# Turning the head outputs on VectorE instead of TensorE in the first stack of a two-stack kernel

## The reference

```
h = rms_norm(x, gain);  proj = h @ w_in          # q, k, v, z of two kinds of attention, and two gates
DA: 8 heads, two maps each:  a = softmax(q1 k1') - lam * softmax(q2 k2');  o = rms_norm(a @ v) * c
    ua = o * silu(z)                             # 256 columns a head
SB: 16 heads of 128:  w = stick-breaking weights of q k';  ub = (w @ v) * silu(z)
y = sigmoid(gate_a) * (ua @ w_branch_a) + sigmoid(gate_b) * (ub @ w_branch_b)
x = x + y @ w_out
```

## Time and profile before

| what | value |
|---|---|
| median of 3 runs | 3218.58 us (3218.3 to 3219.7) |
| span of the profiled execution | 3216.8 us, 1.8 us less than the median of the runs |
| TensorE busy | 3208.1 us, 100% of the span |
| VectorE busy | 2002.6 us, 62% |
| ScalarE busy | 1666.2 us, 52% |
| GpSimd busy | 502.8 us, 16%; 424.81 us of it in the first 1650 us |
| TensorE transposes of U, L2075 | 128, in 32 groups of four |
| granted TensorE clock | 1.000 over the whole span |

### The profile page before, as it was taken

One profiled execution on the slowest core, in us unless ns is written; L12 is line 12 of the kernel. 1 busy time (PEld: TensorE's weight loads), 2 busy tenths in 40 slices (PEclk: granted clock), 3 DMA queues, 4 the chain that ended last, 5 costly groups with the idle time before them and its releaser, 6 DMA issues.

```text
span 3216.8 us, 47383 instructions
## 1 busy us (share of the span) xinstructions
PE 3208.1 (100%) x16986; PEld 2760.8 (86%) x16986; DVE 2002.6 (62%) x2267; ACT 1666.2 (52%) x2326; POOL 502.8 (16%) x425
## 2 busy tenths in 40 slices
PE   9999999999999999999999999999999999999999
PEld 7888888888888888888888888888889999999997
DVE  6667655555544555666654555444458888688975
ACT  5445455555444444454455555444446557465663
POOL 4544500000000003445410000000001000100000
PEclk9999999999999999999999999999999999999999
DMA  6555555554555555455555455555564444544454
GB/s 241 174 171 183 173 174 169 176 171 168 191 195 192 193 196 185 164 187 171 170 178 179 165 175 174 183 192 194 192 209 166 155 144 147 181 160 162 145 182 146
DMA packets 157289, 568.95 MB, mean 177 GB/s; under 512 B 17552, under 2 KB 19744, under 8 KB 156768
## 3 DMA queue, kind: packets, MB, share of 16 engines
q1 hardware_dynamic: 155680, 558.00, 52.1%
q0 software_dynamic: 1488, 9.26, 0.8%
HBM read 565.09 MB, written 2.10 MB: 176 GB/s over the span
## 4 chain that ended last, share of the span: by engine, by line
PE 99%; POOL 1%; DVE 0%; issue 0%; ACT 0%; DVEq 0%; POOLq 0%; ACTq 0%
PE acc L1955 23%; PE acc L1957 23%; PE acc L1956 23%; PE acc L2343 5%; PE acc L2344 5%; PE acc L2345 5%; PE acc L2270 1%; PE acc L2268 1%; PE acc L2269 1%; PE work L2018 1%; PE work L2406 1%; PE work L2314 1%; PE work L2317 1%; PE work L2318 1%; PE work L2373 0%; PE work L2432 0%
## 5 line engine op out<-in xcount | busy, mean ns | idle before, releaser
L1181 DVE TENSOR_TENSOR w_lo<-raw,w_hi 128x1024 fp32r<-128x1024 f32 x1055 | 1400.2, 1337 | 992.2 <-ACT w_hi L663 858.4
L663 ACT ACTIVATE w_hi<-raw 128x1024 fp32r<-128x1024 f32 x831 | 873.4, 1057 | 903.9 <-PE acc L1957 898.7
L1955 PE MATMUL acc<-w_hi,hT_hi 128*128 128x512 f32 x2560 | 1013.7, 396 | 1.4 <-DVE hT_lo L1187 1.4
L1957 PE MATMUL acc<-w_hi,hT_lo 128*128 128x512 f32 x2560 | 998.1, 390 | 0.0
L1956 PE MATMUL acc<-w_lo,hT_hi 128*128 128x512 f32 x2560 | 996.6, 389 | 0.0
L1957 PEld LDWEIGHTS acc<-w_hi,hT_lo 128*128 128x128 f32 x2560 | 480.5, 188 | 102.6
L1955 PEld LDWEIGHTS acc<-w_hi,hT_hi 128*128 128x128 f32 x2560 | 481.0, 188 | 96.2 <-issue 1.7
L1956 PEld LDWEIGHTS acc<-w_lo,hT_hi 128*128 128x128 f32 x2560 | 481.4, 188 | 95.5
L677 ACT ACTIVATE w_hi<-raw 128x1024 fp32r<-128x1024 f32 x224 | 236.1, 1056 | 260.1 <-PE acc L2345 200.1
L2343 PE MATMUL acc<-h_hi,w_hi 128*128 128x272 f32 (+1 forms) x1088 | 318.5, 293 | 0.0
L2344 PE MATMUL acc<-h_lo,w_hi 128*128 128x272 f32 (+1 forms) x1088 | 311.9, 287 | 0.0
(11 more groups left out here) (381 smaller groups left out, 3830.4 us busy)
## 6 DMA issues: line engine op xcount, KB each, us to landing
raw<-weights SPq DMA_DIRECT2D x1056, 512.0 KB, 3.4
mat<-mats POOLq DMA_DIRECT2D x2, 1536.0 KB, 8.7
X<-x_in SPq DMA_DIRECT2D x8, 256.0 KB, 8.1
GB_rows<-rows POOLq DMA_DIRECT2D x1, 2048.0 KB, 9.9
out<-out_rows SPq DMA_DIRECT2D x8, 256.0 KB, 2.6
par<-params POOLq DMA_DIRECT2D x2, 640.0 KB, 5.4
cst<-consts POOLq DMA_DIRECT2D x1, 704.0 KB, 6.2
cst<-consts POOLq DMA_DIRECT2D x1, 552.0 KB, 5.1
```

The source lines that it names most:

```text
L663: act.activation(w_hi[:, slot, :], raw[:, slot, :], ACT.Copy).then_inc(hi_ready, 1)
L1181: dve.tensor_tensor(w_lo[:, s % RING, :], raw[:, s % RING, :], w_hi[:, s % RING, :], ALU.subtract)\
L1955: pe.matmul(o, stat[0][:, kc, token], hi, start=(kc == 0), stop=False)
L1957: ins = pe.matmul(o, stat[1][:, kc, token], hi, start=False, stop=(kc == KC - 1))
```

## The change

TensorE's `turn_u` is removed, and with it the wait of `turn_qk` for `u_lo`. VectorE gets a `turn_u` of its own directly after `make_u`: sixteen stream transposes for each unit. Transpose (i, j) reads 32 partitions of U, with 32 columns of each of four blocks (two column halves by two token tiles), turns each 32 x 32 block, and writes 32 x 128 values to the partitions 32 j of a new SBUF tile `UT`. `UT` lies where the score tile `SM` is, which holds nothing that is still needed at that time. U is stored in another order of its free axes, and `make_u` of an SB pair is two instructions instead of one. `u_hi` waits for all sixteen transposes and reads `UT` in SBUF instead of PSUM, and so does `u_lo`.

The diff at its core:

```diff
+        sm_at = mem.at
         SM = mem.place("SM", [P, 2, 384])
+        UT = mem.place("UT", [P, 4, 4, 32], at=sm_at)
-        U = mem.place("U", [P, NT, 256])
+        U = mem.place("U", [P, 2, NT, P])
...
             def u_hi(m):
-                act.wait_ge(uT_turned, m["n"] + 1)
+                act.wait_ge(uT_turned, 16 * (m["n"] + 1))
-                act.activation(dst[:, bass.ds(2 * m["i"], 2), :], work[:, 0, :].rearrange("p (c n) -> p c n", c=2), ACT.Copy)\
-                    .then_inc(uT_hi, 1)
+                act.activation(dst[:, bass.ds(2 * m["i"], 2), :].rearrange("p c (t i r) -> p (c t) i r", t=NT, i=4),
+                               UT[:, :, :, :].rearrange("p i b r -> p b i r"), ACT.Copy).then_inc(uT_hi, 1)
...
+            def turn_u(m):
+
+                dve.wait_ge(u_ready, 2 * (m["n"] + 1))
+                for i in range(4):
+                    for j in range(4):
+                        dve.transpose(UT[32 * j:32 * j + 32, i, :, :],
+                                      U[32 * i:32 * i + 32, :, :, 32 * j:32 * j + 32].rearrange("p c t n -> p (c t) n")).then_inc(uT_turned, 1)
...
             def u_lo(m):
-                dve.tensor_tensor(lo[:, c, :], work[:, 0, :].rearrange("p (c n) -> p c n", c=2), hi[:, c, :], ALU.subtract)\
-                    .then_inc(uT_lo, 1)
+                tokens = "p c (t i r) -> p (c t) i r"
+                dve.tensor_tensor(lo[:, c, :].rearrange(tokens, t=NT, i=4), UT[:, :, :, :].rearrange("p i b r -> p b i r"),
+                                  hi[:, c, :].rearrange(tokens, t=NT, i=4), ALU.subtract).then_inc(uT_lo, 1)
...
                 split(u, 12, 13 + late)
                 if prev:
                     make_u(prev)
+                    turn_u(prev)
                 split(u, 13 + late, 16)
...
-                pe.wait_ge(uT_lo, m["n"])
                 for a in range(4):
...
-            def turn_u(m):
-                pe.wait_ge(u_ready, 2 * (m["n"] + 1))
-                for c in range(2):
-                    for t in range(NT):
-                        o = c * SEQ + t * P
-                        ins = pe.transpose(work[:, 0, o:o + P], U[:, t, c * P:c * P + P], ident)
-                ins.then_inc(uT_turned, 1)
...
-                halves(u, hT, 9 + late, 13 + late)
-                if prev:
-                    turn_u(prev)
-                halves(u, hT, 13 + late, 16)
+                halves(u, hT, 9 + late, 16)
```

More of the change, by code:

```diff
@@ L689, in layer_start @@
                     act.wait_ge(const_set, 2)
-                    act.activation(small[:, 90:91], U[:, 0, 0:1], ACT.Copy)
+                    act.activation(small[:, 90:91], U[:, 0, 0, 0:1], ACT.Copy)
                     act.wait_ge(set_loaded, 32)
@@ L1290, in make_u @@
                     for t in range(NT):
-                        dve.scalar_tensor_tensor(U[:, t, :], work[:, 1, 256 * t:256 * t + 256], o_rstd[:, t:t + 1],
-                                                 ZG[:, t, :], ALU.mult, ALU.mult).then_inc(u_ready, 1)
+                        dve.scalar_tensor_tensor(U[:, :, t, :], work[:, 1, 256 * t:256 * t + 256].rearrange("p (c n) -> p c n", c=2),
+                                                 o_rstd[:, t:t + 1], ZG[:, t, :].rearrange("p (c n) -> p c n", c=2),
+                                                 ALU.mult, ALU.mult).then_inc(u_ready, 1)
                 else:
                     dve.wait_ge(av_ready, m["n"] + 1)
-                    dve.tensor_tensor(U[:, :, :], work[:, 1, :].rearrange("p (t n) -> p t n", t=2), ZG[:, :, :], ALU.mult)\
-                        .then_inc(u_ready, 2)
+                    for t in range(NT):
+                        dve.tensor_tensor(U[:, :, t, :], work[:, 1, 256 * t:256 * t + 256].rearrange("p (c n) -> p c n", c=2),
+                                          ZG[:, t, :].rearrange("p (c n) -> p c n", c=2), ALU.mult).then_inc(u_ready, 1)
+            def turn_u(m):
[4 more added lines that the diff above has]
+                                      U[32 * i:32 * i + 32, :, :, 32 * j:32 * j + 32].rearrange("p c t n -> p (c t) n")).then_inc(uT_turned, 1)
             def u_lo(m):
@@ L1989, in first_step @@
                     for _ in range(FIRST_WARM):
-                        pe.matmul(work[:, 3, 0:256], U[:, 0, 0:P], U[:, 1, :], start=True, stop=True)
+                        pe.matmul(work[:, 3, 0:256], U[:, 0, 0, :], U[:, 1, :, :], start=True, stop=True)
                     pe.wait_ge(set_loaded, 32)
```

## The result

The changed kernel takes 3273.05 us (median of 5 runs, 3269.04 to 3278.15), the kernel before 3218.58 us (5 runs, 3217.68 to 3219.7). The ratio is 1.017, with a 95% interval from 1.016 to 1.0181: 54.5 us slower. The profiled execution has a span of 3271.3 us.

A forecast was written before the change was run, and what follows sets the result against it. TensorE was taken to bound the kernel, holding 99% of the chain. 14 DA steps losing 3.33 us each (46.6) less 8.8 us saved in 18 other steps gave +37.8 us, a 3256 us median, range 3222 to 3278 us.

The forecast's parts named there:

- main case: Whole kernel: 246 ns a transpose delays split 13 and half 0 in DA steps; 3246 to 3264 us, chance 40%.
- What TensorE saves, and the SB steps: TensorE: four transposes gone, about 0.49 us a step; VectorE's turns hidden in 18 steps, which save 8.8 us.
- What VectorE gets: VectorE after make_u: sixteen transposes at 246 ns each, 3.9 us together (2.1 to 6.1).
- Split 13 late: DA steps: transposes and GpSimd's turn delay split 13, so TensorE starts half 13 at 243.0 instead of 240.52.
- `u_lo` among the blocked: DA steps, VectorE: with both inputs in SBUF, u_lo takes turns with GpSimd, over 2 us instead of 0.68.
- Half 0 late: DA steps, TensorE: split 0 ends at 252.4, due at 251.16, so half 0 waits and starts at 252.5.
- The sum: Whole kernel: 14 DA steps lose 3.33 us each, 46.6 us, less 8.8 saved elsewhere: +37.8 us, 3256 us median.
- QN late: Rival, turn_qk in DA steps: two more VectorE instructions ahead of L533 delay QN; 1.2 us a step, 3227 us, chance 10%.
- All hidden, faster if VectorE is free by 239.1: Rival, DA steps: at 138 ns a transpose TensorE does not wait; all 32 steps save, -15.7, 3203 us, chance 12%.
- Milder: Rival, DA steps: at about 200 ns a transpose half 0 starts 1.73 us later; +15.4, 3234 us, chance 22%.
- Dearer: Rival, DA steps: at 380 ns a transpose half 0 starts 4.35 us later; +52, 3271 us, chance 10%.

The follow-up runs named there:

- sb_only: Changed kernel with the change undone in the 14 DA steps, where TensorE turns U again: 3210.95 us against 3218.79 for the kernel before.
- wide_short: Changed kernel with one 128 x 512 transpose and GpSimd's rotation cut to 8 columns a head (values wrong): 3201.55 us against 3218.03 for the kernel before.
- same_q: Changed kernel, each transpose writing to the 32 partitions it reads from (turned blocks in wrong places): 3254.08 us, one run.
- wide: Changed kernel with one 128 x 512 transpose instead of sixteen narrow ones (turned values in wrong places): 3274.97 us, ratio 1.0175 to the kernel before.
- warm: Changed kernel plus 12 matmuls on dead data between halves 12 and 13 of the 14 DA steps: 3252.66 us, ratio 1.0106 to the kernel before.
- cross_runs: Changed kernel, four transposes in a row reading one partition group and all writing the next group (turned blocks in wrong places): 3256.84 us, one run.
- moved: Changed kernel, in DA steps VectorE's turn of U behind splits 13 and 14, ScalarE's hi copy of half 15 ahead of u_hi: 3240.52 us.
- hi_first: Kernel before, with only ScalarE's order changed in DA steps, hi copy of half 15 ahead of u_hi: 3228.51 us, ratio 1.0032.

## Why the prediction was right, and where its size was off

The kernel got slower, in the place and by the queue that were named; 3273 us lies in the range, but above the main case's own 3246 to 3264. That it lies inside is partly luck: the upper end, 3278, was set for a dearer transpose, and what filled the room was the clock. By its steps:

- **What TensorE saves, and the SB steps.** 0.49 us a step and 8.8 us in the 18 other steps were forecast; an SB step got 0.47 us shorter, sb_only gained 7.8 us, and wide_short the whole at 16.5. Right.
- **What VectorE gets.** I took 246 ns a transpose, from the stream shuffle. It is 334 ns, inside the bounds of 130 and 380. The sixteen are 5.3 us instead of 3.9. The row of the shuffle could not show it: it has all 128 partitions and stands alone, and the price here is one of neighbours on different groups (0.33 us), without which it is 0.19 to 0.24. An estimate by the Trainium skill's 75 ns an instruction and 1.0417 ns a column (Vector Engine (DVE) Microarchitecture Reference, "Measured stream behaviour on trn2") gives 208 ns each and 3.3 us. The trace of the change does not agree with 208 ns each; that of same_q does within a row of four (190 to 240 ns, 207 in the mean). Counting the transposes as free beside GpSimd was right (0.74 us for L528).
- **Split 13 late.** Forecast 243.0 for 240.52, 2.5 us; measured 3.03. The transposes are 1.4 us longer and the wait only 0.5, because in the main case VectorE then stands 0.9 us behind GpSimd's L525; ending later, it found its turn within 0.2 us (split 13 starts at 253.22 and frees half 13 at 254.52).
- **`u_lo` among the blocked.** Right: 2.38 us for 0.68, as the Trainium skill's exclusive lock (SBUF — State Buffer, "SBUF: two separate sides") has it, and wide shows every rotation waiting one VectorE instruction.
- **Half 0 late.** Forecast 1.3 us more; in the changed kernel it does not wait in the 12 steps with a low clock, because TensorE comes later itself. With the clock kept up it does, by 0.2 us (warm, and the two steps above). The forecast was too long because it set four GpSimd instructions between split 13 and split 0 (L526, L527, L529, L533, by the old lines); with transposes that end later the last L526 is done before split 13 gets its turn, and three stand there (L529, L531, L535 in the rows above).
- **The sum.** The forecast of 3.33 us a DA step has no term for the clock; it stood only in the last sentence of the prediction, as something that would make it wrong. It is the term that failed: 28.0 us of the 54.5, shown by the windows and by warm. Without it, the waits, saved turns and SB steps add up to 42.4 - 6.9 - 8.5 = +27 us, less than the forecast 37.8; with the clock kept up and the wait of half 0 back (warm) it is +33.9. A DA step was forecast at 51.3 us: it is 51.0 where the clock stays up, and 52.5 in the mean.
- **The rivals.** "QN late" was given 1.2 us a step and 3227 us. Its mechanism is real and much larger: 3.0 us and 3275 us in wide, with 0.7 us of transposes (below the lower bound of 2.1), because VectorE, once free, takes a turn at each change and not only two more. "All hidden, faster if VectorE is free by 239.1" is refuted by the same run: there VectorE is free at about 237.7 of that frame, and neither of its two conditions holds, a `u_lo` that is not blocked and a GpSimd that keeps its 251.38. "Milder" needed under 225 ns a transpose and falls with the 334. "Dearer" has nearly the measured number, 3271 us, but by other terms: 380 ns a transpose and 4.35 us a DA step in waits alone, where warm shows 3.05.

## What to carry to other kernels

Before moving work from the engine that bounds to one that is idle a third of the time, look at the free time at that place in the step and at everyone who shares something with the receiver. Here the receiver had 2.5 us in hand where it needed 5.3, and cutting that to 0.7 was no better (wide, 3275 us): its extra turns then held GpSimd back. Price a wait of TensorE at more than its length: to a wait of 2.9 us the low clock added 2 us in the mean, of which 1.5 came back when the wait was filled. And make the change only where there is slack: 18 of 32 steps gave 7.8 us.

## What the runs showed of the hardware

- Stream transposes of 32 x 128 fp32 start 0.19 us apart when neighbours read the same group of 32 partitions and write the same group (0.24 after the first), also when these two groups differ; when the group read or the group written changes, the next one starts 0.03 us after the end of the one before: 0.29 us after the start of one that lasts 0.26, and 0.33 us apart where it changes each time and each lasts 0.30. GpSimd's instructions beside them keep their minimum (0.74 us). One of 128 x 512 is 0.71 us, and the next instruction starts after 0.63 us.
- TensorE's granted clock fell from 1.00 to 0.50 in or within 1.3 us after 12 of the 14 waits of 2.9 us (changed kernel), 13 of the 14 of 3.0 us (wide), 6 and 9 of the 14 of 2.2 us (same_q, cross_runs), and none of the 14 of 1.65 us (moved). In the changed kernel it came back after 3 to 6 us of unbroken matmuls. What decides between two waits of the same length stays open here.
- Two engines that take turns at a shared resource can be slowed by giving one of them less to wait for: a mere reorder on ScalarE made the kernel before 10.4 us slower (hi_first).
